# Adding the experts' rows to x1 in memory by an accumulating indirect transfer, in place of storing them and summing them at the end

## What is computed

```python
def hybrid_layer(x, ...):
    ...
    x = x + g1[:, None, :] * mix                      # this is x1 in the kernel
    h = modulate(rms_norm(x, norm2_w), sh2, sc2)      # h2
    idx, gw = grouped_route(h, w_router, router_bias)   # TOP_K = 2
    y = routed_experts(h, idx, gw, w_gate, w_up, w_down)
    return x + g2[:, None, :] * y

def expert_block(xb, e):
    hb = jax.nn.silu(xb @ w_gate[e]) * (xb @ w_up[e])
    return hb @ w_down[e]

return rms_norm(x, final_norm_w)                      # after the layer
```

## Time and profile before

| what | us |
|---|---|
| median of three runs | 3084.88 |
| the profiled execution's own time | 3082.7 |
| its span, first to last instruction | 3080.6 |
| time outside the span | 2.1 |

### The profile page before, as it was taken

One profiled execution on the slowest core, in us unless ns is written; L12 is line 12 of the kernel. 1 busy time (PEld: TensorE's weight loads), 2 busy tenths in 40 slices (PEclk: granted clock), 3 DMA queues, 4 the chain that ended last, 5 costly groups with the idle time before them and its releaser, 6 DMA issues.

```text
span 3080.6 us, 34900 instructions
## 1 busy us (share of the span) xinstructions
PE 2752.9 (89%) x12582; PEld 2232.0 (72%) x12582; DVE 2396.4 (78%) x1910; ACT 1572.8 (51%) x1507; POOL 541.0 (18%) x432
## 2 busy tenths in 40 slices
PE   2799999999898687999965999999999999999990
PEld 2577777777576565778854888888888888888870
DVE  5879989986847475444446999999999999999987
ACT  5322222222121663332333777778777787877762
POOL 0000000000201010100010232233223323322320
PEclk8899999999999698999987999999999999999995
DMA  9733333334845526555546989999899999999998
GB/s 333 257 102 109 97 101 95 109 98 128 273 152 197 174 74 236 174 183 188 201 169 188 357 362 371 381 391 384 345 364 372 397 397 373 369 365 383 382 368 365
DMA packets 245967, 798.14 MB, mean 259 GB/s; under 512 B 27984, under 2 KB 122464, under 8 KB 174348
## 3 DMA queue, kind: packets, MB, share of 16 engines
q1 hardware_dynamic: 201186, 632.14, 54.4%
q0 software_dynamic: 34144, 130.07, 12.4%
q10 hardware_dynamic: 10570, 35.05, 2.9%
HBM read 755.14 MB, written 87.11 MB: 273 GB/s over the span
## 4 chain that ended last, share of the span: by engine, by line
PE 37%; issue 8%; DVE 7%; DMA 5%; ACT 4%; SPq 0%; DVEq 0%; POOL 0%; ACTq 0%; POOLq 0%
PE ps L1867 4%; PE ps L1868 4%; PE ps L1872 4%; DVE wlo L1581 4%; PE ps L1563 4%; PE ps L1561 4%; PE ps L1562 4%; PE ps L1766 3%; PE ps L1768 3%; PE ps L1767 3%; ACT whi L1571 3%; DMA wraw_o<-in_w_out_dram 2%; DMA gp<-modg_d 1%; ACT L1993 1%; PE ps L1854 1%
## 5 line engine op out<-in xcount | busy, mean ns | idle before, releaser
L1581 DVE TENSOR_TENSOR wlo<-wraw,whi 128x2048 fp32r<-128x2048 f32 x444 | 1005.9, 2286 | 100.7 <-ACT whi L1571 92.5
L1571 ACT ACTIVATE whi<-wraw 128x2048 fp32r<-128x2048 f32 x444 | 851.6, 1919 | 268.5 <-PE ps L1563 135.6
L1561 PE MATMUL ps<-whi,xhi 128*128 128x512 f32 x1184 | 475.5, 402 | 0.0
L1563 PE MATMUL ps<-whi,xlo 128*128 128x512 f32 x1184 | 463.6, 392 | 0.0
L1562 PE MATMUL ps<-wlo,xhi 128*128 128x512 f32 x1184 | 461.8, 390 | 0.0
L708 PE MATMUL ps<-hh,wih 128*128 128x512 f32 x1056 | 336.9, 400 | 14.9 <-DVE wil L696 14.9
L708 PE MATMUL ps<-hl,wih 128*128 128x512 f32 x1056 | 330.4, 394 | 0.0
L708 PE MATMUL ps<-hh,wil 128*128 128x512 f32 x1056 | 329.9, 393 | 0.0
L1037 DVE SCALAR_TENSOR_TENSOR acc<-u,vcur,acc 128x1024 f32<-128x1024 f32 x240 | 308.3, 1284 | 8.0
L1563 PEld LDWEIGHTS ps<-whi,xlo 128*128 128x128 f32 x1184 | 222.4, 188 | 48.5
L690 ACT ACTIVATE wih<-wraw_i 128x1024 fp32r<-128x1024 f32 x72 | 76.1, 1057 | 348.0 <-PE ps L708 303.9
(11 more groups left out here) (379 smaller groups left out, 4318.5 us busy)
## 6 DMA issues: line engine op xcount, KB each, us to landing
wraw<-in_w_gate_dram SPq DMA_DIRECT2D x148, 1024.0 KB, 7.0
wraw<-in_w_up_dram SPq DMA_DIRECT2D x148, 1024.0 KB, 8.3
wraw<-in_w_down_dram SPq DMA_DIRECT2D x148, 1024.0 KB, 7.5
wm<-in_w_mod_dram POOLq DMA_DIRECT2D x88, 512.0 KB, 4.1
wraw_i<-in_w_in_dram SPq DMA_DIRECT2D x72, 512.0 KB, 4.4
wraw_o<-in_w_out_dram SPq DMA_DIRECT2D x128, 256.0 KB, 3.5
wmA<-in_w_mod_dram SPq DMA_DIRECT2D x54, 512.0 KB, 5.2
y<-ybuf_d SPq DMA_DIRECT2D x16, 1024.0 KB, 11.3
```

The costliest lines, as they stand in the source:

```text
L1561: pe.matmul(dst, xhi[:, t, :], whi[:, s, w], start=(t == 0), stop=False)
L1563: last = pe.matmul(dst, xlo[:, t, :], whi[:, s, w], start=False, stop=(t == KT - 1))
L1571: act.activation(whi[:, spl(m), :], wraw[:, raw(m), :], ACT.Copy).then_inc(s_whi, 1)
L1581: dve.tensor_tensor(wlo[:, spl(m), :], wraw[:, raw(m), :], whi[:, spl(m), :].bitcast(F32), ALU.subtract).then_inc(s_wsp[raw(m)], 1)
```

## The change

The scatter of each item no longer stores its rows in `ybuf_d` but adds them to `x1_d`, with the token as index (`gix`), by the same kind of transfer with `compute_op=ALU.add`. A token's two rows are in different items, and a scatter is issued only after the one before has landed, as before. The final stage no longer reads `ybuf_d`: after the last scatter SyncE loads the eight tiles of `x1_d`, each into its own buffer `x1f` (which lies where `whi`, `wlo` and the rest lay, so no slot need come free); ScalarE squares them as they land, VectorE scales them in place, and ScalarE stores from there. The early loads of x1, the loads of y1 and y2, and the 16 additions are gone, and with them the waits for buffers of `of`, `y1` and `y2`.

```diff
@@ buffers
-            y1 = place("y1", [P, 3, D], F32, 0)
-            y2 = place("y2", [P, 3, D], F32, 24 * KB)
-            of = place("of", [P, 2, D], F32, 48 * KB)
+            x1f = place("x1f", [P, TT, D], F32, 0)
@@
-            xf = place("xf", [P, 2, D])
@@
             def x1_last(j):
-                return xf[:, j, :] if j < 2 else wraw[:, (FREED[j - 2] + 1) % NRAW, :]
+                return x1f[:, j, :]
@@ SyncE
                     sp.dma_start(frow[:], bcast(final_norm_w, D)).then_inc(s_fr, 16)
-                    for j in range(TT):
-                        if j >= 2:
-                            m = FREED[j - 2]
-                            sp.wait_ge(s_wsp[raw(m)], raw_turn(n, m) + 1)
-                        sp.dma_start(x1_last(j), x1_d[j * P:(j + 1) * P, :]).then_inc(s_xf[j], 16)
                     sp.wait_ge(s_os, 16 * n + 16)
                     for j in range(TT):
-                        b = j % 3
-                        if j >= 3:
-                            sp.wait_ge(s_sum3, j - 2)
-                        sp.dma_start(y1[:, b, :], ybuf_d[j * P:(j + 1) * P, :]).then_inc(s_y1[b], 16)
-                        sp.dma_start(y2[:, b, :], ybuf_d[SEQ + j * P:SEQ + (j + 1) * P, :]).then_inc(s_y1[b], 16)
+                        sp.dma_start(x1_last(j), x1_d[j * P:(j + 1) * P, :]).then_inc(s_xf[j], 16)
@@ GpSimd
                     def scatter(i):
                         pool.wait_ge(s_or, i + 2)
-                        pool.tensor_copy(oixc[:], oix[:, ds(i, 1)]).then_inc(s_oixc, 1)
+                        pool.tensor_copy(oixc[:], gix[:, ds(i, 1)]).then_inc(s_oixc, 1)
                         pool.wait_ge(s_oixc, i + 1)
                         pool.tensor_tensor(pace[:], ones[:, 0:1], ones[:, 0:1], ALU.mult)
-                        pool.indirect_dma_start(out=ybuf_d[:, :],
+                        pool.indirect_dma_start(out=x1_d[:, :],
                                                 out_offset=bass.IndirectOffsetOnAxis(ap=oixc[:], axis=0),
                                                 in_=orow[:], in_offset=None,
-                                                bounds_check=y_rows, oob_is_err=False).then_inc(s_os, 16)
+                                                bounds_check=x_rows, oob_is_err=False, compute_op=ALU.add).then_inc(s_os, 16)
@@ ScalarE
                     for j in range(TT):
-                        act.wait_ge(s_sum3, j + 1)
+                        act.wait_ge(s_xf[j], 16)
...
                         if j >= 1:
                             act.wait_ge(s_of3, j)
-                            act.dma_start(out[(j - 1) * P:j * P, :], of[:, (j - 1) % 2, :]).then_inc(s_out[(j - 1) % 2], 16)
+                            act.dma_start(out[(j - 1) * P:j * P, :], x1_last(j - 1)).then_inc(s_out[(j - 1) % 2], 16)
@@ VectorE
-                    def combine(j):
-                        dve.wait_ge(s_y1[j % 3], 32 * (j // 3) + 32)
-                        order(dve.tensor_tensor(y1[:, j % 3, :], y1[:, j % 3, :], y2[:, j % 3, :], ALU.add))
-                        dve.wait_ge(s_xf[j], 16)
-                        dve.tensor_tensor(x1_last(j), x1_last(j), y1[:, j % 3, :], ALU.add).then_inc(s_sum3, 1)
...
+                    dve.wait_ge(s_fr, 16)
+                    for j in range(TT):
                         dve.wait_ge(s_std3, j + 1)
                         order(dve.reciprocal(rst3[:, j:j + 1], rst3[:, j:j + 1]))
-                        if j >= 2:
-                            dve.wait_ge(s_out[b], 16 * (j // 2))
-                        dve.scalar_tensor_tensor(out=of[:, b, :], in0=x1_last(j), scalar=rst3[:, j:j + 1],
+                        dve.scalar_tensor_tensor(out=x1_last(j), in0=x1_last(j), scalar=rst3[:, j:j + 1],
                                                  in1=frow[:], op0=ALU.mult, op1=ALU.mult).then_inc(s_of3, 1)
-
-                    dve.wait_ge(s_fr, 16)
-                    combine(0)
-                    for j in range(1, TT):
-                        combine(j)
-                        finish(j - 1)
-                    finish(TT - 1)
```

More of the change, by code:

```diff
@@ L1445, in hybrid_layer @@
             later_at = place_at[0]
-            xf = place("xf", [P, 2, D])
-            assert ys_off + place_at[0] <= 229368
-            place_at[0] = later_at
             def t3(name, a, b=None):
@@ L1726, in scatter @@
                         pool.wait_ge(s_or, i + 2)
-                        pool.tensor_copy(oixc[:], oix[:, ds(i, 1)]).then_inc(s_oixc, 1)
+                        pool.tensor_copy(oixc[:], gix[:, ds(i, 1)]).then_inc(s_oixc, 1)
                         pool.wait_ge(s_oixc, i + 1)
                         pool.tensor_tensor(pace[:], ones[:, 0:1], ones[:, 0:1], ALU.mult)
-                        pool.indirect_dma_start(out=ybuf_d[:, :],
+                        pool.indirect_dma_start(out=x1_d[:, :],
                                                 out_offset=bass.IndirectOffsetOnAxis(ap=oixc[:], axis=0),
                                                 in_=orow[:], in_offset=None,
-                                                bounds_check=y_rows, oob_is_err=False).then_inc(s_os, 16)
+                                                bounds_check=x_rows, oob_is_err=False, compute_op=ALU.add).then_inc(s_os, 16)
                     x_rows = pool.value_load(nitems_d[0:1, 1:2], min_val=0, max_val=SEQ - 1)
-                    y_rows = pool.value_load(nitems_d[0:1, 2:3], min_val=0, max_val=2 * SEQ - 1)
                     pool.wait_ge(s_xz, 1)
@@ L2025, in _ @@
                             act.wait_ge(s_of3, j)
-                            act.dma_start(out[(j - 1) * P:j * P, :], of[:, (j - 1) % 2, :]).then_inc(s_out[(j - 1) % 2], 16)
+                            act.dma_start(out[(j - 1) * P:j * P, :], x1_last(j - 1)).then_inc(s_out[(j - 1) % 2], 16)
                     act.wait_ge(s_of3, TT)
-                    act.dma_start(out[(TT - 1) * P:TT * P, :], of[:, (TT - 1) % 2, :]).then_inc(s_out[(TT - 1) % 2], 16)
+                    act.dma_start(out[(TT - 1) * P:TT * P, :], x1_last(TT - 1)).then_inc(s_out[(TT - 1) % 2], 16)
                     for b in range(2):
@@ L2387, in _ @@
                     order = Order(dve, o_p7)
-                    def combine(j):
-                        dve.wait_ge(s_y1[j % 3], 32 * (j // 3) + 32)
-                        order(dve.tensor_tensor(y1[:, j % 3, :], y1[:, j % 3, :], y2[:, j % 3, :], ALU.add))
-                        dve.wait_ge(s_xf[j], 16)
-                        dve.tensor_tensor(x1_last(j), x1_last(j), y1[:, j % 3, :], ALU.add).then_inc(s_sum3, 1)
-                    def finish(j):
-                        b = j % 2
+                    dve.wait_ge(s_fr, 16)
+                    for j in range(TT):
                         dve.wait_ge(s_std3, j + 1)
                         order(dve.reciprocal(rst3[:, j:j + 1], rst3[:, j:j + 1]))
-                        if j >= 2:
-                            dve.wait_ge(s_out[b], 16 * (j // 2))
-                        dve.scalar_tensor_tensor(out=of[:, b, :], in0=x1_last(j), scalar=rst3[:, j:j + 1],
+                        dve.scalar_tensor_tensor(out=x1_last(j), in0=x1_last(j), scalar=rst3[:, j:j + 1],
                                                  in1=frow[:], op0=ALU.mult, op1=ALU.mult).then_inc(s_of3, 1)
-                    dve.wait_ge(s_fr, 16)
-                    combine(0)
-                    for j in range(1, TT):
-                        combine(j)
-                        finish(j - 1)
-                    finish(TT - 1)
         ph23.close()
```

## The result

The changed kernel takes 3072.29 us in the median of six runs (3068.69 to 3081.30), the kernel before on the same chips 3085.86 us. The ratio of the runs is 0.9949, with a 95% interval of 0.9926 to 0.9972: 0.5% faster, about 16 us. Forecast were 3059.5 us and a range of 3056 to 3070, so the sign was right and the gain about 10 us short. The forecast's first rival, in which stretches of large items stall, had put the time at 3067 to 3074 with a chance of 0.08.

A forecast was written before the change was run, and what follows sets the result against it. TensorE was taken to bound the loop, a serial chain and then VectorE the end. Final stage ending at 3054.2, last scatter +0 and loop +1 gave a 3055.2 us span, 25.4 less; forecast 3059.5 us, range 3056 to 3070.

The forecast's parts named there:

- first rival: Loop: in two stretches of large items each period is 1 to 2 us longer; 3067 to 3074 us, chance 0.08.
- The final stage: After the last scatter: bound by DMA, 16.78 MB in 40.0 us at 419 GB/s plus 1.9 us for the ends.
- rule in the Trainium skill: Final stage: HBM side binds at about 358 GB/s, so 46.9 us for 16.78 MB; 3066.4 us; the forecast rejected it.
- The price of an added row: Loop scatters: an added row holds its DMA engine 0.629 us against 0.310 for a plain one.
- The charge of 1 us for the loop: Loop: 1 us charged for all additions, between ends of 0 and 38.9 us.
- A mean item hides its 1.1 us: Loop: a mean item's extra DMA time of 1.1 us hides; only full items exceed the period, by 1.9 us.
- the free time from the earlier trace: Loop: DMA time free per period from its mean share: 3.2 us light, 2.9 from 1898, 0.7 fullest.
- M: Theory of the experiments, for the loop: the 16 DMA engines together are overloaded where many rows move.
- TensorE is still three pieces behind: Loop, 1898 to 2078 us: TensorE runs three weight pieces behind ScalarE, so the weights' lead takes up the excess.
- The last scatter: End of the loop: dearer addition against early x1 loads gone, net +0 us, bounded by 0 and +3 us.
- The wait of `orow`: Loop: next `orow` waits for the scatter's landing, about 12 us of 29.1, 17 us to spare.
- the third rival: Loop: DMA engines become its bound, 38.9 us longer if pushed back in full, kernel 3098 us; chance 0.05.

The follow-up runs named there:

- experiments 1 and 2: Changed kernel with each item's rows spread over the DMA engines (1: 3062.86 us) or crowded, eight in a row on one engine (2: 3108.44 us).
- 15.4 in the second: Second profile of the changed kernel, repeated unaltered beside the one with rows spread over the DMA engines: 3069.41 us, ratio 0.9948.
- experiment 3: Changed kernel with the scatter's addition left out, a plain store into x1: 3058.42 us, ratio 0.9914.
- the spread store: Kernel before, plain store kept, with an item's rows spread over the DMA engines: 3081.35 us, ratio 0.9987.
- the spread addition's second profile: Changed kernel with rows spread over the DMA engines, timed again beside the unaltered changed kernel: 3061.59 us, ratio 0.9926.

## Why the prediction was wrong

**The final stage: right.** The step from VectorE's seven microseconds a tile to a stage bound by DMA came out: 43.4 us against 41.9, VectorE and ScalarE half idle, 16.78 MB. The 1.5 us that were missing lie in a slower start and in a dip to 295 GB/s at about 3041 us, after the first stores have joined the loads; in the five other executions with this stage it takes 42.9 to 43.1 us from the first load to the end. Of the rule in the Trainium skill that would have put the HBM side's limit at 358 GB/s ("DMA: Bandwidth & Descriptors", "Where 436 GB/s comes from"), the stage says no again: 418 to 428 GB/s in six of the seven slices of 5 us from 3030 to 3065 us, and 387 with both ends.

**The price of an added row: right.** 0.629 us against 0.310, read from direct transfers, held for the indirect one: q0's share of the loop rose from 6.3% to 9.4%, by 3.1 points, as "about 3% of the loop" had it.

**The loop: wrong.** The step that failed is "A mean item hides its 1.1 us. Only where items are full does the sum exceed the period". It divided the rows by 16 engines. The rows of an item of 57 are on eight engines, by the map that experiments 1 and 2 bear out, and six of these have the eight rows of a full item: the addition costs them 2.6 us and not 1.1. From this followed the second slip, the free time from the earlier trace rows: a DMA share is the mean of 16 engines, and 0.92 can be eight engines at nearly 1 and eight at less. The charge of 1 us for the loop measured 11.7 us in the first profile and 15.4 in the second. The place was named rightly by the first rival ("five periods from 1898, some five around 2475": the long ones begin at 1934 and at 2483), and its time (3067 to 3074) holds the measured one, but its reason was wrong, so that this was luck: it took them for stretches with much to move, and M, which says that, fell.

**The lead of the weights.** "TensorE is still three pieces behind" was to absorb what is late. ScalarE's timeline (in brackets the idle time and who ended it) shows how that ends once the pieces are late in each turn:

```profile
1948.27 1.92 ACT L1566 ACTIVATE whi<-wraw 128x2048 fp32r<-128x2048 f32 x1 [0.80 <-PE ps L1558]
1952.75 1.92 ACT L1566 ACTIVATE whi<-wraw 128x2048 fp32r<-128x2048 f32 x1 [2.56 <-DMA wraw<-in_w_gate_dram]
...
1962.36 1.92 ACT L1566 ACTIVATE whi<-wraw 128x2048 fp32r<-128x2048 f32 x1 [2.78 <-DMA wraw<-in_w_up_dram]
```

The first is still a wait for TensorE, 0.80 us; the next two are for weights, 2.56 and 2.78 us, so the lead is gone, and over the stretch the loop runs at about the busiest engine's pace (37.06 us a period against the estimate of 37.3).

**The last scatter** was taken as +0 and was +0.7 us, the net of two larger terms. With the plain store and without the early loads of x1 it lands in 3.2 us (experiment 3), so the loads gone give 2.3 us and the addition, four rows on one engine, takes 3.0. **The wait of `orow`** (12 us of landing forecast, 12.2 in the median, 14.8 at most) and **GpSimd** came out as said. Two figures beside the sum are a little off: 2 MB at 419 GB/s are about 5 us and not 5.5, and the 3098 of the third rival counts the loop's 1 us twice. Neither enters the forecast.

**The last item** is longer by 1.6 us, which was in no term. In the windows 3001 to 3006 and 3006 to 3010 us, where TensorE stood still for 2.3 and then 0.7 us ahead of the last products, the granted clock is 0.79 and 0.83, means over stretches at the lower level (0.5, 1.2 GHz) and the full one (1.00, 2.4 GHz), where the kernel before kept 1.00:

```profile
3001.00:3006.00 5.00, 2.92 (x9) 2.32 (x10) 3.53 (x4) 3.51 (x3) 0.00 (x0) 0.79 0.68 143
3006.00:3010.00 4.00, 4.00 (x16) 3.18 (x15) 2.90 (x2) 0.00 (x0) 0.00 (x0) 0.83 0.00 0
```

Other executions have it too, those with the plain store among them (25.7 us for this stretch in the spread store), and some have not (23.1 us in the spread addition's second profile). So it comes and goes with the execution, with the addition or without it.

## What to carry to other kernels

The mean share of the DMA engines is a poor bound where a transfer fills only part of the partitions. Count the work of the busiest engine, weights included, for one turn of the loop, and hold that against the turn; here 37.3 us against 36.07 told what a mean share of 0.90 to 0.92 hid. Where rows fill a tile only in part, place them so that neighbouring rows fall on different engines: one table of slot numbers gave back 8 to 9 us, and the wrong one cost 36. And a term that hides under slack deserves its own check of who has that slack.

## What was unexpected of the hardware

An addition into memory by an indirect transfer takes 0.63 us of a DMA engine for a row of 8192 bytes, as by a direct one, where a plain row takes 0.31. Where its rows are spread it costs little else. The queue of the weights moved its 439.5 MB in 86.7% of 1262.2 us before and in 84.8% of 1273.9 us after, so its packets became no longer; the loop with plain stores and the loops with spread additions differ by 0.8 to 1.9 us for nearly 2000 added rows; and GpSimd's instruction takes 3.49 us in place of 2.89. And the landing time of such a transfer follows the rows of its busiest engine: the same 10 rows take 3.5, 6.2 or 8.4 us, by which partitions they lie on.
